# The recurrence of a two-block model laid out in another order, with two triangular inversions on two engines

## The reference

```
S_t = S_{t-1} diag(w_t) + (S_{t-1} a_t) b_t^T + v_t k_t^T        (state 64 x 64 for each head)
y_t = S_t r_t                      with a_t = -kk_t, b_t = kk_t * a_t (per channel), kk = k*k_k normalised per head
y = groupnorm(y) * ln_w + ln_b + sum(r*k*r_k) * v;   out = (y * g) @ wo
```

## Time and profile before

| What | Value |
|---|---|
| median of 3 runs (lowest, highest) | 3222.15 us (3219.92, 3224.57) |
| the profiled execution's own time | 3219.93 us |
| its span, first to last instruction | 3218.1 us |
| PE busy over the span | 2887.2 us, 90% |
| DVE busy | 1484.2 us, 46% |
| POOL busy | 1484.8 us, 46% |
| mean granted TensorE clock | 0.911 of full |
| the recurrence block, first PE instruction to last DVE instruction | 270.17 to 454.59 us |

### The profile page before, as it was taken

How to read it: one execution, slowest core, us unless ns; L and a number is a source line. 1 busy time by engine, 2 the same in 40 slices (tenths; PEclk the granted TensorE clock), 3 DMA queues, 4 the chain that set the end, 5 groups by cost and what they waited for, 6 DMA issues and landing times. The chain is left out here.

```text
span 3218.1 us, 38131 instructions
## 1 busy us (share of the span) xinstructions
PE 2887.2 (90%) x15212; PEld 2220.6 (69%) x15212; DVE 1484.2 (46%) x2071; ACT 776.1 (24%) x1380; POOL 1484.8 (46%) x479
## 2 busy tenths in 40 slices
PE   4998789999999988899999999997959799999998
PEld 4776677888878833367888887774623377778777
DVE  5566366755222046527555272354078567210351
ACT  4543312211021232213111221221133212111210
POOL 3753435777766400046777442331200067654474
PEclk9999789999999856689999899998969999999999
DMA  4211245666322100015555221131222242221121
GB/s 203 105 66 47 74 173 200 237 222 222 118 87 84 65 0 0 0 40 196 222 209 191 84 79 73 65 118 56 82 69 87 91 185 91 79 95 66 53 91 66
DMA packets 81157, 345.13 MB, mean 107 GB/s; under 512 B 26361, under 2 KB 38649, under 8 KB 43521
## 3 DMA queue, kind: packets, MB, share of 16 engines
q1 hardware_dynamic: 65472, 238.90, 20.3%
q10 hardware_dynamic: 15552, 104.34, 8.8%
HBM read 312.79 MB, written 30.41 MB: 107 GB/s over the span
## 5 line engine op out<-in xcount | busy, mean ns | idle before, releaser
L484 POOL TENSOR_TENSOR whi<-wraw,con_sb 128x2048 fp32r<-128x2048 f32 x170 | 613.8, 3611 | 1625.4 <-PE ps L540 1410.9
L486 POOL TENSOR_TENSOR wlo<-wraw,whi 128x2048 fp32r<-128x2048 f32 x170 | 804.2, 4730 | 13.3
L540 PE MATMUL ps<-hh,whi 128*128 128x512 f32 x952 | 373.6, 392 | 9.7 <-DVE hl L1737 5.0
L540 PE MATMUL ps<-hl,whi 128*128 128x512 f32 x952 | 371.9, 391 | 0.0
L540 PE MATMUL ps<-hh,wlo 128*128 128x512 f32 x952 | 371.7, 390 | 0.0
L540 PEld LDWEIGHTS ps<-hh,whi 128*128 128x128 f32 x952 | 179.6, 189 | 47.6 <-DVE hl L1737 5.4
L1940 DVE TENSOR_TENSOR midl<-rsq,midh 128x512 fp32r<-128x512 f32 x64 | 155.4, 2433 | 113.6 <-ACT midh L1902 113.6
L540 PEld LDWEIGHTS ps<-hh,wlo 128*128 128x128 f32 x952 | 179.6, 189 | 37.7
L540 PEld LDWEIGHTS ps<-hl,whi 128*128 128x128 f32 x952 | 179.6, 189 | 37.4
L540 PE MATMUL ps<-midh,whi 128*128 128x512 f32 x512 | 199.9, 390 | 0.0
L540 PE MATMUL ps<-midh,wlo 128*128 128x512 f32 x512 | 199.3, 389 | 0.0
(11 more groups left out here) (398 smaller groups left out, 5572.4 us busy)
## 6 DMA issues: line engine op xcount, KB each, us to landing
wraw<-wst SPq DMA_DIRECT2D x174, 1024.0 KB, 4.8
cond_w<-wcond ACTq DMA_DIRECT2D x68, 1024.0 KB, 4.8
first_w<-wcond SPq DMA_DIRECT2D x8, 1024.0 KB, 19.1
mod_w<-wcond SPq DMA_DIRECT2D x8, 1024.0 KB, 13.5
d_v<-ssb ACTq DMA_DIRECT2D x4, 1536.0 KB, 5.2
d_s<-ssb ACTq DMA_DIRECT2D x4, 1536.0 KB, 5.3
sld<-d_s SPq DMA_DIRECT2D x4, 1536.0 KB, 6.9
vld<-d_v SPq DMA_DIRECT2D x16, 384.0 KB, 3.4
```

What stands on the lines that cost most here:

```text
L484: pool.tensor_tensor(whi[:, s], wraw[:, f], C("zero").broadcast_to([P, BLK]), ALU.add).then_inc(sem("w_high"), 1)
L486: pool.tensor_tensor(wlo[:, s], wraw[:, f], whi[:, s].bitcast(F32), ALU.subtract).then_inc(w_split, 1)
L540: o = e.matmul(ps[:, b, :nt], w[:, k, mc], x[:, k0 + k, t0:t0 + nt], start=first and k == 0 and j == 0, stop=final and k == nk - 1 and j == 2)
```

## The change

In the block of the mixes the copy of r into PSUM is dropped, and DVE multiplies r in place:

```diff
-                    dve.wait_ge(*r_copied.at(g + 1))
-                    dve.tensor_tensor(chunked(rx), chunked(ps[:, 7]), at, ALU.mult).then_inc(*r_scaled.inc())
+                    stepped(dve.tensor_tensor(chunked(rx), chunked(rx), at, ALU.mult))
...
-                    if g:
-                        act.wait_ge(*r_scaled.at(g))
-                    act.activation(ps[:, 7], r_sb[:, g], ACT.Copy).then_inc(*r_copied.inc())
```

In the recurrence, tiles are placed anew so that all eight fronts can come first, `tt` and `tmp` exist twice (`tn` once), only one tile `tb` is left for the bonus operand, and only the bonus parts of pairs 0 to 3 go through DRAM. PE's order (ACT's follows it):

```diff
-                for hf in HALVES:
-                    for p in range(4 * hf, 4 * hf + 4):
-                        front(p)
-                    for p in range(4 * hf, 4 * hf + 4):
-                        middle(p)
-                        if p % 2:
-                            back(p // 2)
-                merged(0, "Y1", "T12")
+                for p in range(KT):
+                    front(p)
+                for p in range(6):
+                    middle(p)
+                    if p % 2:
+                        back(p // 2)
+                merged(0, "Y1")
+                middle(6)
+                merged(0, "T12")
+                middle(7)
+                back(3)
                 for p in range(4):
                     corrected(p)
...
                 for c in range(1, 7):
                     state(0, c)
-                    if c == 3:
+                    if c == 1:
                         merged(1, "Y1")
-                    elif c == 4:
+                    elif c == 2:
                         merged(1, "T12")
-                    elif c >= 5:
-                        corrected(c - 1)
-                corrected(6)
-                corrected(7)
+                    else:
+                        corrected(c + 1)
```

DVE inverts the first half between its middles; POOL inverts the second half alone, with the same 60 steps:

```diff
+                def inverse_steps(s0, s1):
+                    tt, tmp = tts[0], tmps[0]
+                    for s in range(s0, s1):
+                        n = 31 - s
+                        part = tmp[:, :s * n].rearrange("p (i j) -> p i j", j=n)
+                        row = tt[:, s:s + 1, s + 1:].broadcast_to([P, s, n])
+                        col = tt[:, 0:s, s:s + 1].broadcast_to([P, s, n])
+                        stepped(dve.tensor_tensor(part, row, col, ALU.mult))
+                        stepped(dve.tensor_tensor(tt[:, 0:s, s + 1:], tt[:, 0:s, s + 1:], part, ALU.add))
...
                 bonus_part(0)
-                bonus_part(1)
-                for p in range(4):
+                for p in range(KT):
                     front(p)
-                for p in range(4):
+                dve.wait_ge(*blk_in.at(16))
+                for p, (s0, s1) in enumerate(((1, 7), (7, 13), (13, 20), (20, 31))):
+                    inverse_steps(s0, s1)
+                    if p == 3:
+                        stepped(dve.memset(tts[0].rearrange("p s t -> p (s t)")[:, 0::33], 1.0))
+                        dve.tensor_copy(tn, tts[0].rearrange("p s t -> p t s")).then_inc(*inverted[0].inc())
                     middle(p)
-                for p in range(4, 8):
-                    front(p)
-                for p in range(4, 8):
+                for p in range(4, KT):
                     middle(p)
```

POOL waits for the first inverse to be written out before it makes its turned copy (`pool.wait_ge(*inv_out.at(32))`). SP's list:

```diff
                 blocks_out(0)
                 blocks_in(0)
+                blocks_out(1)
+                blocks_in(1)
                 bonus_out(0)
                 bonus_out(1)
-                blocks_out(1)
                 inverse_back(0)
-                bonus_out(2)
-                bonus_out(3)
                 inverse_back(1)
```

More of the change, by code:

```diff
@@ L1171, in stepped @@
                     pool.wait_ge(*inverse_step.at(inverse_step.made))
[L1172 to L1182, removed]
+                tt, tmp = tts[1], tmps[1]
+                pool.wait_ge(*blk_in.at(32))
+                for s in range(1, 31):
+                    n = 31 - s
+                    part = tmp[:, :s * n].rearrange("p (i j) -> p i j", j=n)
+                    row = tt[:, s:s + 1, s + 1:].broadcast_to([P, s, n])
+                    col = tt[:, 0:s, s:s + 1].broadcast_to([P, s, n])
+                    stepped(pool.tensor_tensor(part, row, col, ALU.mult))
+                    stepped(pool.tensor_tensor(tt[:, 0:s, s + 1:], tt[:, 0:s, s + 1:], part, ALU.add))
+                stepped(pool.memset(tt.rearrange("p s t -> p (s t)")[:, 0::33], 1.0))
+                pool.wait_ge(*inv_out.at(32))
+                pool.tensor_copy(tn, tt.rearrange("p s t -> p t s")).then_inc(*inverted[1].inc())
                 pool.wait_ge(*by_dve.at(nth["YC", 3, 1][1]))
@@ L1283, in fg @@
                 def fg(p, i, what, c2):
-                    return annex[rows(c2), 2 * (p % 4) + i // 4, P * (i % 4) + CH * what:][:, :CH]
+                    return annex[rows(c2), 2 * (p % 4) + i // 4, P * (i % 4) + CH * (1 - what):][:, :CH]
                 def corrected(p):
                     begin(("FG", p, 0), ("FG", p, 1), after=(("T12", p // 2),))
-                    step = AT_t(p) - AV_t(p)
+                    step = AV_t(p) - AT_t(p)
                     for turn in range(2):
@@ L1294, in corrected @@
                                        item(arena[rows(c2), A_t(p)], i),
-                                       arena[rows(c2), AV_t(p):AT_t(p) + 1:step, CH * i:CH * i + CH])
+                                       arena[rows(c2), AT_t(p):AV_t(p) + 1:step, CH * i:CH * i + CH])
                                 if turn == 1 and k == 3:
@@ L1472, in y_squares @@
                                    scale=1.0 / 64).then_inc(*y_rooted.inc())
-                for hf in HALVES:
-                    for p in range(4 * hf, 4 * hf + 4):
-                        front(p)
-                    for p in range(4 * hf, 4 * hf + 4):
-                        middle(p)
-                        if p % 2:
-                            back(p // 2)
-                chunk_matrices(0)
-                chunk_matrices(1)
+                for p in range(KT):
+                    front(p)
+                for p in range(6):
+                    middle(p)
+                    if p % 2:
+                        back(p // 2)
+                merged(0, "Y1")
+                middle(6)
+                merged(0, "T12")
+                middle(7)
+                back(3)
+                corrected(0)
+                merged(1, "Y1")
+                merged(1, "T12")
+                corrected(1)
                 y_squares(0)
```

126 lines of the change are left out of this document (65 added, 61 removed).

## The result

Before: 3223.02 us, median of 6 runs (3219.92 to 3224.57). After: 3239.65 us, median of 6 (3235.04 to 3247.38). Ratio 1.0056 [1.0043, 1.0070]. The two profiled executions took 3219.93 and 3239.22 us: 19.3 apart, against the 12.9 of the forecast; in medians it is 16.6. The slower side and the place are as forecast, the size is 4 to 6 us more: 3239.65 lies in the wide range of the forecast (3219 to 3243) and just above the narrow one (3226 to 3239).

The account below looks back on a forecast made before the run. PE, busy 90% of the span, was taken as the bound, so its gaps count outside the recurrence, which was read by itself. 19.5 - 1.75 - 1.0 - 4.35 + 0.5 = +12.9 us gave 3232.8 us; range 3219 to 3243.

Parts of the forecast that it names:

- rival 1: DVE's inversion steps are dearer still because their rows are short: back(1) at 346.5, 3244.8 us, from +18 up; chance 0.12.
- Rival 3: DVE/POOL exclusion fades and PE's clock stays at 2.4 GHz from back(1) through the state loop: 3214.5 us; chance 0.10.
- DVE alone: DVE's 60 inversion steps without POOL beside them: 21.4 us in all, 0.14 us each plus 1.07 ns a column.
- Parts 1 and 2: First two of four parts of DVE's inversion, 12 instructions each, ahead of middles: 3.4 and 4.7 us.
- DVE beside POOL: DVE's last 36 inversion instructions alternate with POOL's, both reading SBUF twice: 24.1 us instead of 13.3.
- Rival 2: DVE/POOL exclusion fades for short instructions: back(1) at 323.3, 3221.6 us, no change; chance 0.18.
- Back(1): PE product held behind DVE's inversion and middle(3): starts at 334.5 instead of 302.01, after PE idles 17 us.
- Back(1) to corrected(0): PE's products there take 35.9 us at 2.4 GHz, plus 3 for half clock; corrected(0) at 373.4, 19.5 later.
- Corrected(0) to the first transfer: Gains: 1.75 us from corrected(0) in dense PE, 1.0 from DVE no longer meeting POOL's copy, 4.35 in the state loop.
- State loop: From the states' start to the first transfer, with dense new filling: 21.3 us instead of 25.65, so 4.35 back.
- Behind transfer(4): The 51 us from there to the end of the block: same work in the same order, no change.
- Mixes block: ACT's copies go, DVE reads SBUF twice: +0.5 us, between -0.6 and one more wait of 4.6; sign: within 1 us.

Follow-up runs that it names:

- experiment 1: Changed kernel, but POOL starts its inversion only when DVE has ended its own, so the two do not overlap: 3227.24 us, ratio 1.0006 to before.
- experiment 4: Kernel before, but DVE inverts the second half behind its last middle, and Y1, T12 and corrected 4 to 7 fill the state loop earlier: 3219.45 us, ratio 0.9982.
- experiment 2: Changed kernel with the products of DVE's inversion steps in PSUM, so the adds read SBUF only once: 3230.88 us, ratio 1.0017 to before.
- Experiment 3: Changed kernel without DVE's 60 inversion steps (first half's output wrong), diagonal and turned copy kept: 3211.83 us, ratio 0.9961 to before.
- 6: Kernel before with DVE inverting the second half late, behind its last middle, but the mergings in their old places: 3221.27 us, ratio 0.9989.
- experiment 5: Kernel before with the mixes-block edit alone (r multiplied in place from SBUF, ACT's eight copies gone): 3223.95 us, ratio 0.9999.

## Why the prediction came out as it did

Right in its sign, in its mechanism and in the place; its sum was 6.4 us short of the profiled pair. The number alone (16.6 in medians, 19.3 in the pair) is nearer to the foot of rival 1 (from +18 up) than to the forecast's 12.9; what tells the two apart is the trace and experiment 1. Rival 3 falls with the gap of 17.28 us. Its condition, no gap over 4 us, is a limit that no run here shows: in experiment 4 the clock already fell behind 1.90 us of idle. By the prediction's own steps:

- **DVE alone.** Parts 1 and 2 computed 3.4 and 4.7, measured 3.45 (293.08 to 296.53) and 4.80 (299.03 to 303.83). The price of a column held down to 30 columns, and experiment 1 gives it for all parts. The Trainium skill, page Vector Engine (DVE) Microarchitecture Reference, section 5.2, gives 1.30 to 2.51 ns a column for a stream off adjacent pairs on even words, against 1.054 for whole rows. The prediction wrote these as 1.3 to 2.5 times; with 1.75 ns a column its estimate of 3241 would be 3240. The steps on rows of 1 to 30 words with a stride of 32 do not show such a price: 30 columns in 0.19 us and 240 in 0.41 are 1.05 ns a column. The copy of 1024 columns read turned took 1.03 to 1.17 us, against the 1.4 that I had taken.
- **DVE beside POOL.** 24.1 us forecast for parts 3 and 4, 23.6 measured (9.0 and 14.6): one DVE instruction for one of POOL, on average 0.66 apart. The last five or so of part 2 ran beside POOL's first, short ones and lost nothing (303.42). Rival 2, that short instructions slip past, is refuted by DVE's last one: 30 columns, 0.56 us. The Trainium skill, page SBUF — State Buffer, section Who interferes with whom, calls the shared ports an exclusive lock and excepts DVE instructions with at most one SBUF input outside the 2-port modes. The trace agrees on the lock, with DVE's end 0.27 us behind POOL's at 308.87, and on the exception for the adds of experiment 2, at 0.40. Two DVE copies with one SBUF input exclude POOL's instructions, or are held by them, all the same: the turned copy at 332.91, and the copy of 8 columns in the earlier trace rows, which the prediction counts among instructions with both inputs in SBUF though it has one. No run tells in which mode these ran. The forecast did not rest on that row alone.
- **Back(1).** Forecast 64.3 in, measured 65.0; the gap ahead of it 17 and 17.3. POOL started 1.4 later than forecast, counted from the block's start, with no effect on the sum. Half clock behind the gap: forecast 3, measured 2.5.
- **Back(1) to corrected(0): the step that was short.** Forecast 38.9, measured 40.95. Back(1) with its half clock took 6.4 (forecast 6.95), and the two middles and the wait behind it match (343.34 to 351.97 is 8.63, computed 8.61). Back(2) took 5.03 instead of 3.95 up to Y1, of it 0.82 a stall named "issue". Y1 took 4.05 instead of 3.28, with a stall of 1.23 in it. Middle(6) behind that stall ran at a granted clock of 0.50 (361.05 to 365.51) and took some 5.9 instead of 3.37. T12 took 2.2 instead of 3.63. So two errors partly cancel: the sum was said to be all at 2.4 GHz, but its 3.28 and 3.63 come from the earlier trace rows, where the clock was 0.53, and are 1.9 too dear by these rows; back(2), the second stall and middle(6) cost 4.8 more than was put down, nothing of it for stalls. That only 2 us are missing here is in part luck. Experiment 3 has the same second stall at 333.78 (1.23), so it goes with this order of products, not with DVE. What PE's queue does there was not tested.
- **Corrected(0) to the first transfer.** -1.75 and -1.0 forecast, -2.75 measured. State loop: 21.3 and 21.7. Experiments 4 and 6 give its worth a second time (22.1 against 25.1).
- **Behind transfer(4): taken as unchanged, +1.3.** 52.56 us from there to the next block's first product, before 51.24. The states of the second half ran longer at half clock (435.53, 7.57 us against 6.88), the last sums 6.30 against 5.38, and two "issue" stalls were 1.00 and 1.24 us against 0.34 and 0.97.
- **Mixes block: +0.5 forecast, +1.8 in the pair,** of which 0.8 is there already at PE's first spread product (201.63 against 200.79) and 1.3 at DVE's first instruction behind it (203.22 against 201.93), ahead of the edited lines. It is more than the 1 us that the prediction named as its sign. In the other kernels the block starts anywhere from 270.18 to 273.3 us, with and without the edit, and experiment 5 finds no difference.

Sum of the pair: 1.8 + 22.2 - 2.75 - 3.9 + 1.3 = 18.6 of 19.3. Against the forecast 2.7 of the missing us lie between back(1)'s place and corrected(0), 1.3 each in the tail and in the mixes block, 0.4 in the loop; 0.7 of the pair lies outside of these stretches. None of these is the wrong mechanism for the loss, but the stalls named "issue" were put at nothing, and what I took as unchanged is not quite unchanged. Most of what is missing is more "issue" stalls and more half clock.

## What to carry to other kernels

Two engines do not halve a serial chain when both read SBUF twice in each step: the second one only fills the gaps of the first, and whatever stands behind it in its own list pays. Before moving work onto an engine, list what that engine owes others at that moment; here an inversion cost 28 us ahead of the masks, beside POOL's, and one of the same size cost nothing that the runs show behind the last of them, where it made the kernel 0.18% faster than before, together with the new places of the mergings. Price the layout and the load separately (experiment 3 does it with one line), since a change that loses may carry a part worth keeping.

## What was unexpected of the hardware

- The price of exclusion does not shrink with the instruction: DVE's 30 columns cost 0.19 us alone and 0.56 beside POOL, its 240 columns 0.41 and 0.63. What an instruction pays is the rest of POOL's running one, so the dearest place for it is a long row of tiny instructions.
- Whether an instruction that reads SBUF twice is held depends on when it starts: one that starts up to some 0.15 us ahead of the end of POOL's keeps its solo length (198 columns in 0.37 us, experiment 2). And a DVE copy with one SBUF input holds POOL as well (150 columns in 1.16 us).
- The granted clock falls behind short pauses too, and not the same way twice: back(1) took 5.50 us behind 1.90 of idle at a granted clock of 0.69 in experiment 4, and 3.95 behind 1.87 at 1.00 in the kernel before, in the same order of products.
